# Queries and keys per token tile inside the expert stage, expert selection two heads at a time, branch weights in two chunks

## What is computed

```python
h2 = rms_norm(x, norm2) * (1 + sc2) + sh2
q = (h2 @ w_q).reshape(T, 8, 2, 128)                  # 8 heads, two halves; w_q is 1024 x 2048
s = einsum('thsk,snk->thsn', q, sub_keys)             # 128 keys on each side
sv, si = top_k(s, 16)
cand_s = sv[..., 0, :, None] + sv[..., 1, None, :]    # 256 candidates a head
top_s, top_pos = top_k(cand_s, 16)                    # 16 experts a head, 128 a token
idx = take_along_axis(si0 * 128 + si1, top_pos);  g = softmax(top_s)
a = gelu(einsum('tkd,td->tk', u_tab[idx], h2))
x = x + g2 * einsum('tk,tkd->td', g * a, v_tab[idx])
```

## Time and profile before

| | |
|---|---|
| runs | 5095.93, 5098.10, 5099.51 us |
| profiled execution | 5105.13 us, of which the span is 5103.0 |
| mean granted TensorE clock | 0.935 |
| TensorE, VectorE, ScalarE, GpSimd busy | 79%, 62%, 10%, 50% |
| DMA | 1562.73 MB, mean 306 GB/s |
| gathers (q0) / loads (q1) | 1342.34 MB, 69.3% / 217.90 MB, 13.1% of 16 engines' span |
| chain that ended last | PE 36%, DMA 29%, POOL 13%, DVE 12%, issue 7% |
| sample expert stage, layer 0 / 1 | 1202 to 2777 us / 3639 to 5083 us |

### The profile page before, as it was taken

The page is one execution under the profiler, slowest core; times in us unless marked ns, Lnnn a source line. Parts: engine busy times, 40 slices in busy tenths (PEclk is TensorE's granted clock), DMA queues, the critical chain, the costliest instruction groups (busy, mean ns, idle before and its releaser), DMA issues.

```text
span 5103.0 us, 36619 instructions
## 1 busy us (share of the span) xinstructions
PE 4040.7 (79%) x11183; PEld 1858.8 (36%) x11183; DVE 3139.0 (62%) x7049; ACT 527.1 (10%) x1162; POOL 2526.8 (50%) x2570
## 2 busy tenths in 40 slices
PE   8889788897777777777778988899277777777777
PEld 4664343343332333333333544344122222222223
DVE  1155877666666665665555587766866665765553
ACT  1121330110100100000001133001000000000000
POOL 0003355401666666666663244550267676676674
PEclk9889999999899999999999999999599999999999
DMA  8545679829999999999996467982399999999997
GB/s 267 164 127 202 222 263 331 291 67 306 367 399 362 353 393 375 376 402 375 377 402 237 169 231 246 326 310 77 128 386 404 355 382 376 375 393 375 360 409 289
DMA packets 578097, 1562.73 MB, mean 306 GB/s; under 512 B 51104, under 2 KB 246256, under 8 KB 576626
## 3 DMA queue, kind: packets, MB, share of 16 engines
q0 software_dynamic: 368640, 1342.34, 69.3%
q1 hardware_dynamic: 208690, 217.90, 13.1%
q10 hardware_dynamic: 576, 0.16, 0.0%
HBM read 1557.44 MB, written 2.79 MB: 306 GB/s over the span
## 4 chain that ended last, share of the span: by engine, by line
PE 36%; DMA 29%; POOL 13%; DVE 12%; issue 7%; DVEq 1%; ACT 1%; SPq 0%; PEldq 0%; PEld 0%; POOLq 0%; ACTq 0%
DMA rows<-in_peer_v_dram,idx 14%; POOL rows L2067 13%; PE ps L765 11%; DMA rows<-in_peer_u_dram,idx 11%; PE ps L1217 9%; PE ps L1107 4%; DVE rows L1952 3%; PE ps L735 2%; DVE work L1994 2%; PE ps L775 2%; PE ps L810 1%; DMA ring<-in_w_branch_c_dram 1%; PE ps L1110 1%; DMA ring<-in_w_in_dram 1%; DMA ring<-in_w_ada_dram 1%
## 5 line engine op out<-in xcount | busy, mean ns | idle before, releaser
L1217 PE MATMUL ps<-rows,work 128*128 128x512 f32 x4096 | 2016.2, 624 | 652.9 <-DMA rows<-in_peer_v_dram,idx 603.9
L2067 POOL DMA_INDIRECT rows<-in_peer_u_dram,idx x1280 | 1258.0, 983 | 1359.0 <-DVE idx L1945 809.3
L1952 DVE CUSTOM_DVE_ANT_0 rows<-rows,ps 128x1024 f32<-128x1024 f32 x1024 | 1248.4, 1220 | 1075.5 <-DMA rows<-in_peer_u_dram,idx 1062.7
L2067 POOL DMA_INDIRECT rows<-in_peer_v_dram,idx x1280 | 1268.1, 991 | 1190.9 <-DVE work L1994 475.9
L1217 PEld LDWEIGHTS ps<-rows,work 128*128 128x128 f32 x4096 | 735.1, 195 | 1865.2 <-issue 1438.8
L765 PE MATMUL ps<-h_s,ring 128*128 128x512 f32 x1024 | 452.9, 597 | 4.1 <-DMA ring<-in_w_in_dram 4.1
L2031 DVE TENSOR_SCALAR work<-cst,acts,g_w 128x128 f32<-128x128 f32 x1024 | 368.4, 362 | 53.4 <-PE ps L1217 22.8
L1952 DVE CUSTOM_DVE_ANT_0 rows<-rows,work 128x1024 f32<-128x1024 f32 x256 | 312.3, 1223 | 143.6 <-DMA rows<-in_peer_u_dram,idx 136.0
L1994 DVE SCALAR_TENSOR_TENSOR work<-rows,acts,work 128x1024 f32<-128x1024 f32 x254 | 325.3, 1281 | 4.8
L765 PE MATMUL ps<-work,ring 128*128 128x512 f32 (+1 forms) x768 | 273.7, 510 | 53.8 <-DMA ring<-in_w_branch_c_dram 39.2
L765 PEld LDWEIGHTS ps<-h_s,ring 128*128 128x128 f32 x1024 | 196.8, 193 | 255.7 <-issue 250.8
(11 more groups left out here) (286 smaller groups left out, 3015.3 us busy)
## 6 DMA issues: line engine op xcount, KB each, us to landing
ring<-in_w_in_dram SPq DMA_DIRECT2D x72, 1024.0 KB, 10.3
ring<-in_w_ada_dram SPq DMA_DIRECT2D x48, 1024.0 KB, 5.3
ring<-in_peer_wq_dram SPq DMA_DIRECT2D x32, 1024.0 KB, 5.7
rows<-in_peer_u_dram,idx POOLq DMA_INDIRECT x1280, 7.2
rows<-in_peer_v_dram,idx POOLq DMA_INDIRECT x1280, 7.1
ring<-in_w_out_dram SPq DMA_DIRECT2D x16, 1024.0 KB, 11.6
ring<-in_tables_dram SPq DMA_DIRECT2D x10, 1024.0 KB, 8.1
ring<-in_w_branch_c_dram SPq DMA_DIRECT2D x16, 512.0 KB, 11.2
```

Of the source, the lines that this page charges most:

```text
L1217: mm = pe.matmul(y_acc[:, cols], diag[:, e % TOPK, :], rows[:, ROWS + s, cols], start=e == 0, stop=e == EXPERTS - 1)
L1952: dve.tensor_tensor_reduce(rows[:, s, :], rows[:, s, :], tok, 1.0, 0.0, ALU.mult, ALU.add, dots[:, e:e + 1]).then_inc(rows_u_free, 1)
L2067: pool.indirect_dma_start(rows[:, slot0 + s, :], None, table, bass.IndirectOffsetOnAxis(ap=idx[:, t % 2, e:e + 1], axis=0)).then_inc(came[ ...
```

## The change

- `Inst("Q", ...)` is a new kind of work. The sample queries run in three passes per layer, for tile 0, for tile 1 and for tiles 2 and 3; each pass reads all of `peer_wq` again. Only tile 0's first turn, up to its keys, stands ahead of the expert slots; its other turns are placed in slots -5 to 16, tile 1 in slots 20 to 130, tiles 2 and 3 in 135 to 290. A turn is one tile by 512 query columns (two heads): eight matmuls with the tokens as weights, in two halves of four by input rows, since a 1 MB chunk is now 512 rows by 512 columns; then four transposes, a copy ahead of and behind them, and four key matmuls. The prompt queries have the same form.
- The conditioning of layer 1 moves from slots -14 to 9 on to slots 292 to 364, the prompt mixing of layer 1 to 365 to 480, its queries to 481 to 508; the prompt's last norm in layer 1 to 292.
- Experts are chosen for two heads at a time, four groups a tile, in 5 parts each; `idx_ready` counts groups, and a u gather waits for its group only. Parts of the first tile stand in slots -5 to -1, then up to 58; later groups each start 64 slots ahead of their first row, 6 slots apart.
- The prompt's gates take 512 columns at a time, in halves; `half_used` frees the chunk of a first half. The Q and KV columns come together, 416 wide, in halves.
- The stacked branch chunk becomes `("ab", n)` and `("c", n)`, and all chunks now go through the three slots in turn.

```diff
-PARTS = 15
+PARTS = 5
+GROUPS = 4
+PER_GROUP = EXPERTS // GROUPS
-SOFT_PART = 6
-FIRST_PART, PART_STEP = 4, 7
+SOFT_PART = 2
...
+    def query_turns(self):
+
+        return [(j, c) for c in range(GROUPS) for j in self.tiles]
...
+QUERIES_S = [[Inst("Q", l, True, tiles) for tiles in ((0,), (1,), (2, 3))] for l in range(LAYERS)]
...
-INSTS = [INPUT, ADAS[0], PROMPTS[0], SAMPLES[0], ADAS[1], PROMPTS[1], SAMPLES[1]] + LASTS
+INSTS = [INPUT] + [i for l in range(LAYERS)
+                   for i in [ADAS[l], PROMPTS[l], QUERIES_P[l], SAMPLES[l]] + QUERIES_S[l]] + LASTS
...
+    if kind == "Q":
+        turns = i.query_turns()
+        for n, (j, c) in enumerate(turns):
+            pq, half = ("pq", j, c), (("pqb", j, c), None)
+            if n == 0:
+                ring(pq)
+                o.append(half)
+                ring(("pqt", j, c))
+            elif n == 1:
+                ring(pq, ("key",) + turns[0])
+                o.append(half)
+            else:
+                ring(pq, ("pqt",) + turns[n - 1])
+                o.append(half)
+                ring(("key",) + turns[n - 1])
...
-        take(("gate", 0, n), ("full", ("gate", 0, last)), 1 + n % 2)
-        take(("stack", n), ("full", ("branch", 2, last)), 0, 3)
-        take(("gate", 1, n), ("full", ("gate", 1, last)), 2 - n % 2)
-        take(("gate", 2, n), ("full", ("gate", 2, last)), 1 + n % 2)
+    for n, group in enumerate(i.gate_groups()):
+        last = group[-1]
+        for b in range(3):
+            if i.sample:
+                take(("gate", b, n), ("full", ("gate", b, last)))
+            else:
+                take(("gate", b, n, 0), ("half", ("gate", b, n, 0)))
+                take(("gate", b, n, 1), ("full", ("gate", b, last)))
+            if b == 0:
+                take(("ab", n), ("full", ("branch", 1, last)), 2)
+        take(("c", n), ("full", ("branch", 2, last)))
...
+FIRST_SLOT = -PARTS
+def piece_slot(group, part):
+
+    first, step = {0: (FIRST_SLOT, 1), 1: (1, 2), 2: (12, 5), 3: (38, 5)}.get(group, (PER_GROUP * group - 64, 6))
+    return first + step * part
...
+        o += [(done, PLACE[q0, "begin"] - 1)] * 4
+        o += [(done, PLACE[q0, ("key", 0, 0)])] * 2
+        steps = [(FIRST_SLOT, PLACE[q0, ("pqt", 0, 1)]), (FIRST_SLOT + 2, PLACE[q0, ("pqb", 0, 2)]),
+                 (FIRST_SLOT + 4, PLACE[q0, ("key", 0, 1)]), (0, PLACE[q0, ("pqt", 0, 2)]),
+                 (4, PLACE[q0, ("pqb", 0, 3)]), (9, PLACE[q0, ("key", 0, 2)]), (16, PLACE[q0, ("key", 0, 3)])]
...
+        over(q1, 20, 130)
+        over(q2, 135, 290)
         if l + 1 < LAYERS:
...
-            steps = [(-PARTS + 1 + n, PLACE[ada, ("ada", n)]) for n in range(N_ADA)]
-            steps += [(N_ADA + int(share * (SPREAD * SAMPLE_SLOTS - N_ADA)), place) for place, share in mix_share(pr)]
+            over(ada, 292, 364)
+            over(pr, 365, 480)
+            over(qp, 481, 508)
...
+            def half_turn(a, lhs, w, half):
+
+                for k in range(4):
+                    mm = pe.matmul(a[:, :], lhs[4 * half + k], w[:, k, :], start=half + k == 0, stop=half * k == 3)
+                return mm
...
+                pe.wait_ge(h_ready.sem, h_ready.after(mixed, 2 * KC))
...
             def u_row(t, e):
-                if e == 0:
-                    pool.wait_ge(idx_ready, t + 1)
+                if e % PER_GROUP == 0:
+                    pool.wait_ge(idx_ready, GROUPS * t + e // PER_GROUP + 1)
                 gather(t, e, u_rows, 0, rows_u_free, rows_u_in)
 
             def v_row(t, e):
+                if e == 0 and t % TILES == 0:
+
+                    pool.wait_ge(idx_ready, GROUPS * (t + 1))
                 gather(t, e, v_rows, ROWS, rows_v_free, rows_v_in)
```

More of the change, by code:

```diff
@@ L151, in turn_order @@
         ring(*[(name, c) for name in "qKSTV" for c in range(2)], ("Y", 0))
-    for n in range(KC // 2):
+    for group in i.gate_groups():
         for b in range(3):
-            for half in range(two):
-                ring(("gate", b, n * two + half), ("branch", b, n * two + half))
+            for t in group:
+                ring(("gate", b, t))
+                if not s:
+                    o.append((("gateb", b, t), None))
+                ring(("branch", b, t))
     if not s:
@@ L182, in turn_table @@
         ring = 0
-        for name, bank in turn_order(i.kind):
+        for name, bank in turn_order(i):
             places[i, name] = at
@@ L216, in chunk_order @@
         return o
-    take("Q", ("full", ("qk", i.NT - 1)))
-    take("KV", ("full", ("qk", i.NT - 1)))
+    if i.kind == "Q":
+        for c in range(GROUPS):
+            take(("pq", c, 0), ("half", ("pq", c, 0)))
+            take(("pq", c, 1), ("full", ("pq", i.tiles[-1], c)))
+        return o
+    take(("QK", 0), ("full", ("qk", i.NT - 1)))
+    take(("QK", 1), ("full", ("qk", i.NT - 1)))
     take("V", ("full", ("v", i.NT - 1)))
@@ L1359, in mix @@
                 yield from sample_attention(i) if i.sample else prompt_attention(i)
[L1361 to L1362 removed]
+                slots = [(b, t) for group in i.gate_groups() for b in range(3) for t in group]
                 for r, (b, t) in enumerate(slots):
```

601 lines of the change are left out of this document (310 added, 291 removed).

## The result

The changed kernel takes 5133.9 us (median of 5 runs, 5122.5 to 5143.2), the kernel before beside it 5099.5 us (5 runs, 5095.9 to 5112.6): ratio 1.006, 95% interval 1.0046 to 1.0074. It is slower by 34 us where 110 us less were forecast.

The account below looks back on a forecast made before the run. Sample expert stages were taken as set by bytes, TensorE limiting only the hole and mixing. Terms -273 + 135 + 10 + 24 + 25 - 31 = -110 from 5105.1 gave 4995, less 7.0 for the median: 4988 us, range 4890 to 5065.

Parts of the forecast that it names:

- The hole: First query matmul to first u gather: 174.9 and 174.5 us shrink to 38 each, saving 273 us together.
- Branch weights: Gates of sample and prompt mixing: two chunks remove most TensorE waits on weights, -31 us, between 0 and -45.
- Bytes: Sample expert stages: 32.7 MB more in layer 0, 17.8 in layer 1, at 2.67 us per MB, +135 us.
- First rows: Stage start, 24 u rows before the first v row: 70 us with VectorE's added work; +10 us, between -10 and +25.
- best_keys: Expert stages: twelve more VectorE bursts of 5.4 us per layer, 1 us each, +24 us, between 0 and 72.
- the pair's price: Two best_keys bursts close together lose some 6 us in all; 3 us each gave the best_keys term's upper bound, 72.
- The selection's smaller steps: VectorE's selection in the stage: shorter steps, but twenty instead of fifteen; counted as zero.
- More in fewer slots: Layer 1's prompt mixing in slots 365 to 480, TensorE at 91%: three or four stalls, +25 us, between 0 and 60.
- loads that come in unhindered: Stage start: during the first rows the next weights, 4 MB, 10 us, already counted under bytes, load unhindered.
- the starving one: Rival: late-freed row buffers slow whole expert stages to about 345 GB/s, mean under 355 decides; 5195 us, chance 0.10.
- nearly free loads: Rival: weight loads fill idle DMA time in the stages, 135 us shrink to 35, density costs nothing; 4863 us, chance 0.14.
- the hole closed: The opposing rival: hole doesn't close as written, first gather 60 us later in each layer; 5108 us, chance 0.05.

Follow-up runs that it names:

- b_dense: Kernel before, with sample queries and keys no longer counted in the shares that spread the sample mixing over prompt slots: 5162.2 us, ratio 1.012.
- a_share: Changed kernel with the queries' cost (544 units) counted again in the mixing's shares and the wait for the norm moved behind the queries' first entry: 5075.5 us, 0.9946.
- b_split: Kernel before, with the branch matrices in two chunks and all chunks through the three slots in turn, nothing else: 5085.3 us, ratio 0.9972.
- a_share2: As a_share, but with 1088 units instead of 544 counted in the mixing's shares: 5133.0 us, ratio 1.0064.
- a_merge: Changed kernel with the queries of tiles 1, 2 and 3 in one pass, slots 20 to 172, instead of two: 5091.1 us, ratio 0.9981.
- a_nokeys: Changed kernel without best_keys for tiles 1 to 3, which select from tile 0's keys (part of the computation missing): 5105.9 us, ratio 1.0005.
- a_early: Changed kernel with query passes pushed together, layer 1's conditioning in slots 212 to 300 and its prompt mixing in 301 to 480: 5132.7 us, ratio 1.0057.
- a_all: Changed kernel with 544 units counted, one query pass for tiles 1 to 3, layer 1's conditioning and prompt mixing in slots 175 to 480: 4991.0 us, 0.9785.
- a_spaced: Changed kernel with best_keys of tiles 1 to 3 cut into four pieces at places of their own: 5108.0 us, ratio 1.001.
- a_all_sp: a_all with best_keys cut into four pieces as well: 5005.3 us, ratio 0.9806.

## Why the forecast was wrong

By its own steps, against the profiled executions (errors: measured less forecast):

- **The hole: right.** -273 forecast, -284 measured; 32.7 and 32.8 us left where the steps summed to 38. Of the 38, the first 4 (the wait for all of h) fall ahead of the first query matmul and so into the mixing of the table: there 5.9 us became 10.7. So the steps in the hole make 34 against 32.7.
- **Branch weights: the step that failed.** The forecast had TensorE's waits of 19.2 and 19.9 us turn into time saved in the sample mixing, -23, and took nothing else of the mixing as changed. It grew by 36.6 and 41.6 us: an error of +101 us, most of the whole. The step took a wait at its full length as time saved, and took the rest of the mixing at nothing without a reason. Two things were missing. First, the place of the mixing among the prompt tile's slots depends on a list of work that the change shortens; b_dense shows that this alone costs 24 + 36 us, and a_share gives 23 + 21 back. Second, behind the weights stands VectorE with the expert rows: b_split gains only 13 of 23 us and shows the new wait, 28 us; in the changed kernel TensorE's idle time at gates and branches is 29.4 us against 29.0. The prompt's part was -14 (forecast -8), and -22.6 when done alone.
- **Moved queries: a missed neighbour.** Part of the hole was cover. The first query matmuls ran beside the prompt tile's last gathers and its output; now they stand behind them (22 us behind the last gather in a_share and a_share2, 7 us ahead of it before). This is part of the +101: the wait for the prompt's output is 10.7 us in layer 0 and 9.1 in layer 1.
- **Bytes: right.** 620 and 555 MB against 622 and 558; a_merge gives 43 us for 16.8 MB where 2.67 us per MB makes 45 (37 of the 43 in the stages).
- **First rows: right.** 24 u rows took 66.3 and 66.8 us, forecast 70; layer 1 lost 19 (forecast 22), layer 0 gained 5 (forecast 0).
- **best_keys: right.** +24 forecast, 28 by a_nokeys; the second burst cost 4.7 us where the pair's price made 5. The selection's smaller steps aren't seen apart.
- **More in fewer slots: mis-sized.** Layer 1's stage has +80.7, where bytes, first rows and bursts make 48 + 22 + 12, less 5 as half of what was taken off for loads that come in unhindered, 77. Layer 0's has +162.1 against 194 - 77 = 117: 45 us more, on top of the 25 put down for crowding, so 70, more than the 60 of its bound. The working asked whether the work fits into slots 365 to 480 (TensorE 91% full) and priced three or four stalls of 8 us. It took 1.80 us for an expert's y matmuls, from the query matmuls of the earlier trace rows; the earlier trace rows have 1.96, which makes 95%. TensorE's waits on weights are 42 us in the changed kernel's stage 0 against 21 before, in the conditioning's slots too; but a_early is without them and its stage 0 is only 6.5 us shorter, so their length is not the price of the crowding. Spreading on merged passes gives 41 back in the stage. What is left of the 70, some 30 us, no run tells apart; a_all's stage 0 is still 92 us longer than before's, of which bytes make 65 (24.3 MB) and bursts up to 14.

The errors add up: +101 in the mixing, +49 in the stages, -11 in the hole, -6 in the prompt's mixing, +2 in the turn: +135, which is 25.2 - (-110). None of the rivals was it: the stages ran at 357 and 364 GB/s, above the 355 of the starving one (in layer 0 barely), far below the 390 of nearly free loads, and the hole closed. The range was too narrow because none of its cases let the sample mixing grow: the diff names only its weights, and the term for them went from 0 to -45.

The rule of the Trainium skill, "SBUF — State Buffer", section "Who interferes with whom" (two-port VectorE work keeps GpSimd from writing descriptors), isn't seen in the new place either: in layer 0's stage, now with keys and finer selection steps in it, a u gather's issue takes 948 ns in the mean and a v gather's 939, against 955 and 953 before. Beside the prompt tile's rows the issues are longer, in both kernels: 1096 (u) and 1093 ns (v) in the mean in the changed one (390 to 960 us; the longest 1989), 1094 and 1158 before. There the dot product (line 2053) and the v side (line 2095) read two operands of 1024 elements from SBUF, while a sample tile's dot product takes one of them from PSUM. GpSimd had over 300 us of idle time in that stretch; no run tells the cause of the longer issues or what they cost.

## What to carry to other kernels

Where a planner spreads work by shares, a piece taken off its list moves everything that stays on it: work out the new places of the work that isn't touched, before any price. A stall on one engine is worth its length only if the engine next in line isn't late by the same amount; ask what the waiting engine finds when it comes sooner. And when passes are moved under a stage that is set by bytes, count megabytes, then look at the stage by halves: the loss was all in the half that got the crowded work. Counting the queries' cost again, merging two passes and spreading the rest gave 58, 43 and 40 us, and turned a loss of 0.6% into a gain of 2.15%.

## What the runs showed of the hardware that was not expected

A burst of VectorE work in front of the dot products costs more when it is long: 5.4 us once costs 1.2 us of the run, a second one right behind 4.7. That the rows under way cover one burst and not two is how I read it; cut into four pieces, the same work gained 26 us in one schedule (a_spaced) and lost 14 in another (a_all_sp), so no rule of pieces follows.

The prompt tile's gathers do not speed up when left alone: 35 in 65 us and 281 GB/s with TensorE idle throughout, against 50 in 100 us with the mixing beside them (336 GB/s with its weights). In the chain a u row takes 5.5 to 8.3 us to land, the dot product takes 1.2 to 1.3, the v side behind it about as long, and the next issue 0.94 to 1.9, with four buffers a table.

And a stall can cost more than itself: in the prompt mixing, 10.6 us of waits less came with 10.5 us less of TensorE busy time for the same matmuls, at a granted clock of 0.90 instead of 0.85.
